# Layer 0's local means on GpSimd between weight splits, and token tiles dealt out among the first modulation groups, in a fused kernel of three transformer layers

## The chip, the cores and the metric

One core of one Trainium2 chip. The metric is the device time of one execution in microseconds (us). The kernel before was run three times: median 2811.88 us, 2800.17 to 2812.4 us.

## What is computed

Everything is float32. Two blocks follow each other on 512 tokens of width 1024 (with 256 context tokens in the first block). The first has two layers of adaptive norm, mixer and gated feed-forward; the second has one layer with three kinds of attention and a feed-forward. The change touches two places of layer 0:

```python
def adaln(cond, w, b):                      # cond: c, and c_ctx; w: 1024 x 6144
    m = jax.nn.silu(cond) @ w + b
    return [m[:, None, i * d:(i + 1) * d] for i in range(6)]

h = rmsnorm(x, g) * (1.0 + scale) + shift   # x: tokens and context, 768 in all

def multiscale_pool(u, w_grp, ch_scale):    # u: 256 of the columns of h @ w_in, 4 groups of 64
    ...                                     # windows of 2, 4, 8, 16 tokens
    d = (win_sum / count - ug).astype(u.dtype)
    y = jnp.einsum("btgc,gcd->btgd", d, w_grp).reshape(B, T, POOL_DIM)
    return y * ch_scale
```

The other columns of `h @ w_in` are 12 query heads and 4 key and value heads, which get a head norm and a rotary embedding before attention. `multiscale_pool` is the first part of what goes into the output projection.

## The kernel before

**Engines.** Each engine runs its own program in order; semaphores tie them. TensorE (PE) does all products. A float32 weight tile (1024 x 128, called a unit) lands in one of four slots of `raw`; ScalarE (ACT) rounds it to `whi` (`upper`, line 918), GpSimd (POOL) computes `wlo = raw - whi` (`lower`, line 782), and PE makes three matmuls per piece (lines 1376 to 1378; 1393 to 1395 for the first two units after a norm). POOL does little else in layer 0. SyncE (SP) issues the weight loads in the planned order, each when its slot of the ring is free. There are four PSUM groups `G[0..3]`, taken in turn by every step of the plan; a step waits until the engine that reads the group's last content has freed it (`gfree`).

**The opening.** PE computes the modulation in groups of 512 columns (`ada`, line 1409, four loads of 512 KB each, straight from `raw`), and turns each group's row into columns (`ada_turn`, line 1422), which Vector (DVE) takes with the bias (`ada_columns`, line 1806). Groups 0 to 3 of layer 0 come in the opening. The order is: group 0, the turned vectors (`vec`), all eight token tiles (`xin`: six transposes each, line 1721; DVE copies the tile into `xT`, line 2239; ACT squares it, line 933; DVE adds the square to `ssq`, line 1825), then groups 1, 2, 3. Then comes norm 0: PE sums `ssq` over partitions (line 1445), ACT takes the root (line 953), DVE the reciprocal (line 1833) and a diagonal (line 1835), PE spreads it (line 1452), DVE and ACT write the normed tiles. ACT's order there: squares, groups 1 to 3, `upper(0)`, `upper(1)`, root.

**The input stage `in0`.** Twelve units: 0 and 1 keys, 2 and 3 the 256 columns of the local means, 4 to 9 queries, 10 and 11 values. Beside units 0 to 7 one more modulation group each (groups 4 to 11) is computed. The plan of step n is:

```python
plan_unit((st, "U", n), ...)            # unit n: three matmuls per piece
plan_aux(("adaT",) + ada[n - 1])        # turn modulation group n-1
plan_ada(*ada[n])                       # modulation group n
... "V", n - 1 / "S", n - 1 / "R", n - 2    # values; sum of squares (head norm); rotation
```

For a query or key unit, ACT copies and squares the product (lines 993 and 997, freeing its PSUM group), PE sums the squares (line 1488), ACT takes the root (line 1012), DVE the reciprocal (line 1879) and the scaled copy (line 1883), PE rotates (line 1496), DVE combines (lines 1894, 1895, 1897).

The local means (`pooling`, lines 2268 to 2281) run on DVE as one block, called after its step n = 5: 22 chained additions, products and subtractions over `upad` (two tiles of 128 channels, 800 padded columns) into `dT`. PE needs them only after the twelve units, in the two products with `poolw` (line 1732); then come `pair_attention`, the output projection and the feed-forward.

Of the kernel before, what the change touches and what calls it, by code (L numbers as in the profile page):

```python
# [13 lines left out]
P = 128  # L14
# [90 lines left out]
def build(nc, A, out):  # L105
    with ExitStack() as ctx:
# [34 lines left out]
        eps = sb("eps", [P, 1])  # L141
        zero8 = sb("zero8", [P, KD])
# [416 lines left out]
        def stage_sems(st, *names):  # L559
            for n in names:  # L560
# [3 lines left out]
                   "silu", "b", "rope1", "icnt", "band", "steps", "cszero", "adasel", "halves", "tri")  # L564
        stage_sems("in0", "pooled", "pooly", "pooldone")
# [76 lines left out]
        def _(sp):  # L642
# [9 lines left out]
            with nc.allow_non_contiguous_dma(reason="small vectors"):  # L652
# [4 lines left out]
                sp.dma_start(mats[:], A["mats"][:, 0:8]).then_inc(PH["set", "cond"], 16)  # L657
# [106 lines left out]
        def _(pool):  # L764
# [95 lines left out]
            def causal_tables():  # L860
# [8 lines left out]
                for head in range(4, 6):  # L869
# [39 lines left out]
        def _(act):  # L909
# [17 lines left out]
            def residual_squares(i, ctx_too):  # L927
                n = T if ctx_too else TX
                for m in range(KD):
                    act.wait_ge(*when((f"res{i}", "x"), m + 1))  # L930
                    if m >= 2:
                        act.wait_ge(*when((f"res{i}", "ssq"), m - 1))
                    act.activation(sq[:, m % 2, 0:n], xT[:, m, 0:n], ACT.Square).then_inc(PH[f"res{i}", "sq"], 1)
# [213 lines left out]
            def wout(l, i, n):  # L1147
                for m in range(KD):
                    act.wait_ge(*product_of(("wout", l, m)))
                    upper(plan["wout", l, m][0] + 2)  # L1150
                    if l == 0 and m < len(ADA_WOUT0):
                        ada(*ADA_WOUT0[m])
                    residual_square(i, m, n)

            def ffn(l, chunks, ranges, last_i):
# [4 lines left out]
                for c, (f0, nf) in enumerate(chunks):  # L1160
# [44 lines left out]
                    for m in range(KD):  # L1205
# [6 lines left out]
                        if last and last_i is not None:  # L1212
                            residual_square(last_i, m, n)
# [46 lines left out]
            ada(0, 0)  # L1260
            residual_squares(0, True)
            act.wait_ge(*auxiliary("vec"))
# [1124 lines left out]
```

## Time and profile before

| | |
|---|---|
| median of 3 runs | 2811.88 us |
| range of the runs | 2800.17 to 2812.4 us |
| the profiled execution | 2806.05 us |
| its span | 2804.3 us |
| its mean granted TensorE clock | 0.959 |
| busy share PE / DVE / ACT / POOL | 92% / 40% / 32% / 27% |

The profile is of one execution; its span leaves out 1.75 us of the execution's own time. A row of a timeline gives when an instruction or a run of like ones began, how long it took, its engine and line, what it writes and reads, and in brackets the idle time of the engine before it and what ended that. "DVEq" and "ACTq" are the engines' sequencers, "PEld" the weight loads into the array.

### The profile page before, as it was taken

How to read it: one execution, taken by the hardware profiler on the slowest of the kernel's cores; microseconds unless marked ns; L12 is line 12 of the kernel's file. 1: busy time of each engine (PE TensorE's matmuls, PEld its weight loads, DVE VectorE, ACT ScalarE, POOL GpSimd, SP SyncE). 2: the span in 40 equal slices, each digit the busy share in tenths (PEclk: the TensorE clock that was granted, in tenths of full speed). 3: DMA queues.
4: the chain of work that ended last, by engine and by line, in shares of the span. 5: the costliest groups of instructions: out<-in, count | busy, mean ns of one | idle time of the engine just before them, and what ended most of it. 6: DMA issues, size and time to landing. Idle time of an engine off the chain costs nothing.

```text
span 2804.3 us, 34798 instructions
## 1 busy us (share of the span) xinstructions
PE 2589.0 (92%) x13587; PEld 2016.5 (72%) x13587; DVE 1128.4 (40%) x1578; ACT 910.0 (32%) x1460; POOL 756.7 (27%) x372
## 2 busy tenths in 40 slices
PE   5978999899999998997699988999989998799998
PEld 3656667688888885783277676888867865688887
DVE  4366641411121124347944644222246355434323
ACT  2224641321121223323344533222234365323322
POOL 1111002122222221320200113444444360344443
PEclk8999999899999998998899999999999998999999
DMA  6540017122222234210100112333323310233332
GB/s 240 174 134 24 1 32 222 48 60 67 60 61 67 60 111 133 77 27 20 55 9 8 34 32 74 98 98 98 90 82 83 89 37 1 61 98 97 98 96 77
DMA packets 345573, 212.58 MB, mean 76 GB/s; under 512 B 37747, under 2 KB 318669, under 8 KB 345442
## 3 DMA queue, kind: packets, MB, share of 16 engines
q1 hardware_dynamic: 328176, 200.97, 24.3%
q10 hardware_dynamic: 17202, 9.72, 1.2%
q8 instruction: 91, 1.49, 0.2%
q14 instruction: 40, 0.33, 0.0%
q0 software_dynamic: 64, 0.08, 0.0%
HBM read 208.58 MB, written 2.16 MB: 75 GB/s over the span
## 4 chain that ended last, share of the span: by engine, by line
PE 75%; DVE 9%; issue 7%; ACT 3%; DMA 3%; POOL 2%; ACTq 0%; SPq 0%; DVEq 0%; POOLq 0%
PE G L1376 19%; PE G L1377 19%; PE G L1378 18%; DVE scr L1879 3%; PE G L1517 2%; PE G L1560 2%; POOL wlo L782 2%; PE G L1536 2%; PE G L1588 2%; PE G L1573 2%; PE G L1527 1%; DMA raw<-in_l_ada_w_dram 1%; PE G L1488 1%; PE G L1409 1%; PE G L1393 1%
## 5 line engine op out<-in xcount | busy, mean ns | idle before, releaser
L782 POOL TENSOR_TENSOR wlo<-raw,whi 128x1024 fp32r<-128x1024 f32 x282 | 681.0, 2415 | 1800.2 <-ACT whi L918 1800.2
L1376 PE MATMUL G<-big_a,whi 128*128 128x512 f32 x2024 | 747.4, 369 | 28.9 <-DVE mod L1806 14.9
L1377 PE MATMUL G<-big_a,wlo 128*128 128x512 f32 x2024 | 734.4, 363 | 0.0
L1378 PE MATMUL G<-big_a,whi 128*128 128x512 f32 x2024 | 731.0, 361 | 0.0
L918 ACT ACTIVATE whi<-raw 128x1024 fp32r<-128x1024 f32 x282 | 298.9, 1060 | 1242.5 <-PE G L1378 1051.8
L1376 PEld LDWEIGHTS G<-big_a,whi 128*128 128x128 f32 x2024 | 383.6, 190 | 106.9 <-issue 29.4
L1377 PEld LDWEIGHTS G<-big_a,wlo 128*128 128x128 f32 x2024 | 383.4, 189 | 63.8 <-issue 6.2
L1378 PEld LDWEIGHTS G<-big_a,whi 128*128 128x128 f32 x2024 | 382.3, 189 | 60.6
L1376 PE MATMUL G<-big_b,whi 128*128 128x512 f32 x832 | 307.5, 370 | 7.3 <-DVE big_b L2194 3.5
L1377 PE MATMUL G<-big_b,wlo 128*128 128x512 f32 x832 | 306.6, 368 | 0.0
L1378 PE MATMUL G<-big_b,whi 128*128 128x512 f32 x832 | 305.4, 367 | 0.0
L1879 DVE RECIPROCAL scr<-scr 128x512 f32<-128x512 f32 (+3 forms) x50 | 201.2, 4023 | 159.6 <-ACT scr L1012 158.8
L2177 DVE TENSOR_TENSOR scr<-G,scr 128x768 f32<-128x768 f32 (+1 forms) x44 | 36.3, 825 | 436.2 <-PE G L1378 422.7
L2131 DVE SCALAR_TENSOR_TENSOR xT<-G,mod,xT 128x512 f32<-128x512 f32 (+1 forms) x96 | 60.6, 659 | 358.6 <-PE G L1378 358.6
L1376 PEld LDWEIGHTS G<-big_b,whi 128*128 128x128 f32 x832 | 156.7, 188 | 41.4 <-DVE big_b L2194 5.2
L1378 PEld LDWEIGHTS G<-big_b,whi 128*128 128x128 f32 x832 | 156.4, 188 | 26.7
L1377 PEld LDWEIGHTS G<-big_b,wlo 128*128 128x128 f32 x832 | 156.7, 188 | 25.5
L2182 DVE TENSOR_TENSOR big_b<-scr,big_b 128x768 f32 (+3 forms) x44 | 99.8, 2269 | 46.4 <-ACT big_b L1178 46.4
L2190 DVE TENSOR_TENSOR scr<-scr 128x512 f32<-128x512 f32 x32 | 79.9, 2497 | 65.7 <-ACT scr L1190 65.7
L2129 DVE TENSOR_TENSOR xT<-G,xT 128x512 f32 (+1 forms) x40 | 27.7, 692 | 173.9 <-PE G L1378 162.4
L1081 ACT ACTIVATE scr<-scr,stat 128x768 f32<-128x768 f32 (+4 forms) x136 | 91.1, 674 | 8.0 <-DVE scr L1966 6.3
L1560 PE MATMUL G<-plain_b 64*128 64x256 f32 (+3 forms) x368 | 76.8, 519 | 12.7 <-DVE scr L1966 5.8
(234 smaller groups left out, 2833.2 us busy)
## 6 DMA issues: line engine op xcount, KB each, us to landing
raw<-in_l_ada_w_dram SPq DMA_DIRECT2D x96, 512.0 KB, 5.3
raw<-in_l_ffn_w_gate_dram SPq DMA_DIRECT2D x44, 512.0 KB, 3.9
raw<-in_l_ffn_w_up_dram SPq DMA_DIRECT2D x44, 512.0 KB, 3.8
raw<-in_l_ffn_w_down_dram SPq DMA_DIRECT2D x32, 512.0 KB, 3.6
raw<-in_w_up_dram SPq DMA_DIRECT2D x32, 512.0 KB, 4.0
raw<-in_w_down_dram SPq DMA_DIRECT2D x32, 512.0 KB, 4.1
raw<-in_w_in_dram SPq DMA_DIRECT2D x28, 512.0 KB, 3.8
raw<-in_l_w_in_dram SPq DMA_DIRECT2D x24, 512.0 KB, 3.9
```

Source lines behind the costliest of these rows:

```text
L782: pool.tensor_tensor(wlo[:, u % 2], raw[:, r % RING], whi[:, u % 2].bitcast(F32), ALU.subtract).then_inc(raw_free[r % RING], 1)
L918: act.activation(whi[:, u % 2], raw[:, r % RING], ACT.Copy).then_inc(hi_done, 1)
L1081: act.activation(p, p, ACT.Exp, bias=stat[:, 0, c:c + 1], scale=-1.0, accum_out=stat[:, 1, c:c + 1]).then_inc(PH[C.st, "prob"], 1)
L1376: pe.matmul(o, whi[:, u % 2, k], rlo[:, k, t0:t0 + w], start=k == 0, stop=False)
L1377: pe.matmul(o, wlo[:, u % 2, k], rhi[:, k, t0:t0 + w], start=False, stop=False)
L1378: mm = pe.matmul(o, whi[:, u % 2, k], rhi[:, k, t0:t0 + w], start=False, stop=k == k_tiles - 1)
L1517: mm = pe.matmul(o, un["q"], kt, start=True, stop=fox is None)
L1560: mm = pe.matmul(C.scores(n, h)[:, c0:c0 + wk], heads[h]["q"], kt, start=True, stop=True)
L1879: release(dve.reciprocal(rs, rs), key)
L2131: ins = dve.scalar_tensor_tensor(out=x, in0=src, scalar=gate(m, q, j, dyn), in1=x, op0=ALU.mult, op1=ALU.add)
L2182: dve.tensor_tensor(alo[:, tile_at(j, 2, b), 0:n], sq[:, b:b + 1, 0:n], ahi[:, tile_at(j, 2, b), 0:n].bitcast(F32), ALU.subtract).then_inc ...
L2190: dve.tensor_tensor(sq[:, b % 2, 0:n], qr[:, b % 2, 0:n], qr[:, b % 2, 0:n], ALU.mult).then_inc(PH[sems, "prod"], 1)
```

## The change

Three edits.

1. The 22 operations of the local means go from DVE to POOL, each waiting for the one before by a new semaphore `in0_pooling`. They are dealt out between the weight splits: two (window sums of tile 0) after `lower(6)`, four after `lower(7)`, six after `lower(8)`, two after `lower(9)`, four after `lower(10)` and four after `lower(11)`, with the semaphore `in0_pooled` set at the end. DVE's block disappears.
2. In the opening the eight token tiles are dealt out: tiles 0 and 1 after modulation group 0, 2 to 4 after group 1, 5 to 7 after group 2, none after group 3, on PE, ACT and DVE alike. On SP only the identity (64 KB) is loaded first; the other seven matrices of `mats` (448 KB) follow the loads of group 0.
3. `root_table()`, a root of one column into `spare`, is put ahead of the first use of each norm's root: in the opening ahead of `upper(0)`, elsewhere beside the first tile of the stage before the norm.

```diff
+        XIN_AFTER = ((0, 1), (2, 3, 4), (5, 6, 7), ())
         for i in range(4):
             plan_ada(0, i)
-            if i == 0:
-                plan_aux("vec")
-                for m in range(KD):
-                    plan_aux(("xin", m))
-            else:
-                plan_aux(("adaT", 0, i - 1))
+            plan_aux(("adaT", 0, i - 1) if i else "vec")
+            for m in XIN_AFTER[i]:
+                plan_aux(("xin", m))
...
-                sp.dma_start(mats[:], A["mats"][:, 0:8]).then_inc(PH["set", "cond"], 16)
+                sp.dma_start(ident, A["mats"][:, 0]).then_inc(PH["set", "cond"], 16)
...
+                sp.dma_start(mats[:, 1:8], A["mats"][:, 1:8]).then_inc(PH["set", "mats"], 16)
...
+            pool_steps = [0]
+
+            def pooled(ins):
+                pool_steps[0] += 1
+                ins.then_inc(PH["in0", "pooling"], 1)
+                pool.wait_ge(PH["in0", "pooling"], pool_steps[0])
+
+            L = UPW
+            pa, pb = ptmp[:, 0], ptmp[:, 1]
+
+            def window_sums(i):
+                u = upad[:, i]
+                pooled(pool.tensor_tensor(pa[:, 1:L], u[:, 1:L], u[:, 0:L - 1], ALU.add))
+                pooled(pool.tensor_tensor(pb[:, 2:L - 1], pa[:, 1:L - 2], pa[:, 3:L], ALU.add))
+
+            def wider_sums():
+                pooled(pool.tensor_tensor(pa[:, 4:L - 3], pb[:, 2:L - 5], pb[:, 6:L - 1], ALU.add))
+                pooled(pool.tensor_tensor(pb[:, 8:L - 7], pa[:, 4:L - 11], pa[:, 12:L - 3], ALU.add))
+
+            def window_means(i, half):
+                rows = slice(HD * half, HD * half + HD)
+                sums = pb if half else pa
+                for t0, w, p0 in ((0, TX, 8), (TX, TC, 24 + TX)):
+                    d = dT[rows, i, t0:t0 + w]
+                    pooled(pool.tensor_tensor(d, sums[rows, p0:p0 + w], d, ALU.mult))
+                    pooled(pool.tensor_tensor(d, d, upad[rows, i, p0:p0 + w], ALU.subtract))
+
             for u in range(0, first["wout", 0, 0] + 2):
                 lower(u)
+                if u == 6:
+                    for i in range(2):
+                        key = ("in0", "U", L0_POOL[i])
+                        pool.wait_ge(gfree[group_of(key) % 4], group_of(key) // 4 + 1)
+                    pool.wait_ge(*when(("set", "icnt"), 16))
+                    window_sums(0)
+                if u in (7, 8, 10, 11):
+                    pool.wait_ge(raw_free[unit_ring[u] % RING], unit_ring[u] // RING + 1)
+                if u in (7, 8):
+                    window_means(0, u - 7)
+                if u == 8:
+                    window_sums(1)
+                if u == 9:
+                    wider_sums()
+                if u in (10, 11):
+                    window_means(1, u - 10)
+                if u == 11:
+                    pool.sem_inc(PH["in0", "pooled"], 1)
...
+            def root_table():
+                act.activation(spare[:], eps[:], ACT.Sqrt)
...
-            ada(0, 0)
-            residual_squares(0, True)
-            act.wait_ge(*auxiliary("vec"))
-            act.dma_start(halves[0:12], A["mats"][0:12, 8]).then_inc(PH["set", "halves"], 16)
-            for i in range(1, 4):
+            for i in range(4):
                 ada(0, i)
+                if i == 0:
+                    act.wait_ge(*auxiliary("vec"))
+                    act.dma_start(halves[0:12], A["mats"][0:12, 8]).then_inc(PH["set", "halves"], 16)
+                for m in XIN_AFTER[i]:
+                    residual_square(0, m, T)
+            root_table()
             upper(0)
             upper(1)
...
+            for i in range(4):
+                if i:
+                    ada_columns(0, i - 1)
+                for m in XIN_AFTER[i]:
...
+            sum_squares(0, KD - 1, T)
+            ada_columns(0, 3)
             modulation_gain(0, 0)
...
-            inputs("in0", S0, L0_V, 12, v0_tile, {5: pooling}, ADA_IN0)
+            inputs("in0", S0, L0_V, 12, v0_tile, None, ADA_IN0)
```

**On POOL, in `in0`.** `wlo` rows are the splits of units; the rows on `plain_b` are the new work (window sums on 128 partitions, means on 64). From the split of unit 8 to that of unit 10, before:

```order
L782 TENSOR_TENSOR wlo<-raw,whi 128x1024 x20
```

and now:

```order
L782 TENSOR_TENSOR wlo<-raw,whi 128x1024
L902 TENSOR_TENSOR plain_b<-plain_b 64x512
L903 TENSOR_TENSOR plain_b<-plain_b 64x512
L902 TENSOR_TENSOR plain_b<-plain_b 64x256
L903 TENSOR_TENSOR plain_b<-plain_b 64x256
L890 TENSOR_TENSOR plain_b<-plain_b 128x799
L891 TENSOR_TENSOR plain_b<-plain_b 128x797
L782 TENSOR_TENSOR wlo<-raw,whi 128x1024
L894 TENSOR_TENSOR plain_b<-plain_b 128x793
L895 TENSOR_TENSOR plain_b<-plain_b 128x785
L782 TENSOR_TENSOR wlo<-raw,whi 128x1024
```

The run of 20 splits is cut after the seventh; this is its densest stretch, with six operations between the splits of units 8 and 9 and two between those of 9 and 10.

**On PE, in the opening.** `raw,cs` is a modulation group, `adasel,arow` its turn, `mats,plain_a` the transposes of token tiles (six each), `mats,ssq` norm 0. Before:

```order
L1721 MATMUL G<-mats,plain_a 128x128 x48
L1409 MATMUL G<-raw,cs 32x512 x8
L1422 MATMUL G<-adasel,arow 128x2 x4
L1409 MATMUL G<-raw,cs 32x512 x8
L1422 MATMUL G<-adasel,arow 128x2 x4
L1409 MATMUL G<-raw,cs 32x512 x8
L1422 MATMUL G<-adasel,arow 128x2 x8
L1445 MATMUL G<-mats,ssq 128x1 x6
```

and now (line numbers of the changed file):

```order
L1767 MATMUL G<-mats,plain_a 128x128 x12
L1455 MATMUL G<-raw,cs 32x512 x8
L1468 MATMUL G<-adasel,arow 128x2 x4
L1767 MATMUL G<-mats,plain_a 128x128 x18
L1455 MATMUL G<-raw,cs 32x512 x8
L1468 MATMUL G<-adasel,arow 128x2 x4
L1767 MATMUL G<-mats,plain_a 128x128 x18
L1455 MATMUL G<-raw,cs 32x512 x8
L1468 MATMUL G<-adasel,arow 128x2 x8
L1491 MATMUL G<-mats,ssq 128x1 x6
```

Groups 1 and 2 have moved ahead of six and three of the eight tiles.

**On ACT, ahead of norm 0.** `arow` is a modulation group's copy, `whi<-raw` the split of units 0 and 1. Before:

```order
L942 ACTIVATE arow<-G 128x512 x3
L918 ACTIVATE whi<-raw 128x1024 x2
L953 ACT_TABLE_LOAD
L953 ACTIVATE scr<-G,eps 128x6
```

and now:

```order
L988 ACTIVATE scr<-xT 128x768 x3
L982 ACTIVATE arow<-G 128x512
L973 ACT_TABLE_LOAD
L973 ACTIVATE spare<-eps 128x1
L963 ACTIVATE whi<-raw 128x1024 x2
L993 ACTIVATE scr<-G,eps 128x6
```

The table load stands ahead of the two splits, and the last three squares stand ahead of the copy of group 3.

## Rows read from the trace of the kernel before

**Rows 1.** The page: busy time, share of span and count of each engine.

```profile
PE 2589.0 (92%) x13587; PEld 2016.5 (72%) x13587; DVE 1128.4 (40%) x1578; ACT 910.0 (32%) x1460; POOL 756.7 (27%) x372
```

**Rows 2.** Windows: length, busy us of PE, PEld, DVE, ACT, POOL, clock, DMA share, GB/s.

```profile
140.00:160.00 20.00, 20.00 (x128) 14.86 (x127) 7.08 (x5) 4.73 (x7) 3.93 (x2) 1.00 0.61 185
160.00:180.00 20.00, 5.07 (x15) 3.39 (x14) 19.17 (x23) 2.96 (x4) 2.69 (x1) 0.67 0.43 130
```

**Rows 3.** Waits of PE between 140 and 245 us: total, times, longest.

```profile
PE G L1376 <- DVE mod L1806: 14.9, 1, 14.9
```

**Rows 4.** Timeline of DVE: start us, us, the work.

```profile
158.94 0.99 DVE L2268 TENSOR_TENSOR plain_b<-plain_b 128x799 f32<-128x799 f32 x1
...
176.59 0.17 DVE L1806 TENSOR_TENSOR mod<-G,vcol 128x8 f32<-128x8 f32 x1
```

**Rows 5.** The chain that ended last, 176 to 213 us: start us, us, what.

```profile
176.90 0.77 PE G L1376
...
187.16 0.79 PE G L1422 x8
...
203.59 0.40 PE G L1376
...
212.16 1.29 PE G L1488 x4
```

**Rows 6.** Timeline of POOL, 160 to 240 us.

```profile
164.24 2.69 POOL L782 TENSOR_TENSOR wlo<-raw,whi 128x1024 fp32r<-128x1024 f32 x1 [10.06 <-ACT whi L918]
194.50 2.40 POOL L782 TENSOR_TENSOR wlo<-raw,whi 128x1024 fp32r<-128x1024 f32 x1 [27.57 <-ACT whi L918]
...
235.42 2.34 POOL L782 TENSOR_TENSOR wlo<-raw,whi 128x1024 fp32r<-128x1024 f32 x1 [8.17 <-ACT whi L918]
```

**Rows 7.** Groups of POOL's instructions by form: busy us, mean ns.

```profile
L852 POOL TENSOR_TENSOR plain_a<-scr,vrow 128x128 f32<-128x128 f32 x24 | 11.0, 457 | 13.6 <-DVE scr L2048 13.6
```

**Rows 8.** Timeline of POOL: two instructions linked by a semaphore.

```profile
2265.05 1.27 POOL L842 TENSOR_TENSOR plain_a<-plain_a,arow 128x512 f32<-128x512 f32 x1
2266.40 1.49 POOL L841 TENSOR_SCALAR plain_a<-arow 128x512 f32<-128x512 f32 x1
```

**Rows 9.** DVE's line 1895: duration ns min/median/max, first and last start us.

```profile
L1895 DVE TENSOR_TENSOR rt<-plain_b,rope x8: 681/682/2572, 121.4 to 235.7; 128x512 f32<-128x512 f32 x8
```

**Rows 10.** Timeline of DVE, around 200 us.

```profile
200.71 1.02 DVE L1883 SCALAR_TENSOR_TENSOR plain_b<-scr,vcol 128x768 f32<-128x768 f32 x1
```

**Rows 11.** Timeline of ACT, around 202 us.

```profile
202.53 0.80 ACT L997 ACTIVATE scr<-G 128x768 f32<-128x768 f32 x1
```

**Rows 12.** Timeline of PE in the opening.

```profile
23.31 6.49 PE L1721 MATMUL G<-mats,plain_a 128*128 128x128 f32 x42
...
32.86 1.93 PE L1409 MATMUL G<-raw,cs 128*32 128x512 f32 x16 [1.18 <-DVEq L633]
...
38.08 5.80 PE L1409 MATMUL G<-raw,cs 128*32 128x512 f32 x16 [2.05 <-DMA raw<-in_l_ada_w_dram]
...
50.64 1.95 PE L1422 MATMUL G<-adasel,arow 128*128 128x2 f32 x16
```

**Rows 13.** Window of the opening (columns as in rows 2).

```profile
27.00:35.00 8.00, 5.61 (x48) 3.65 (x47) 6.98 (x9) 3.56 (x5) 0.00 (x0) 1.00 0.01 5
```

**Rows 14.** Timeline of DVE in the opening.

```profile
24.84 0.96 DVE L2239 COPY xT<-G 128x768 f32<-128x768 f32 x1 [0.34 <-PE G L1721]
...
39.14 2.02 DVE L1825 TENSOR_TENSOR ssq<-ssq,scr 128x768 f32<-128x768 f32 x2 [0.23 <-DVE xT L2239]
...
56.66 0.19 DVE L1833 RECIPROCAL scr<-scr 128x6 f32<-128x6 f32 x1
```

**Rows 15.** The page: the weight split's first half on ACT.

```profile
L918 ACT ACTIVATE whi<-raw 128x1024 fp32r<-128x1024 f32 x282 | 298.9, 1060 | 1242.5 <-PE G L1378 1051.8
```

**Rows 16.** Timeline of ACT: table load of norm 0; root of norm 1.

```profile
54.71 1.28 ACT L953 ACT_TABLE_LOAD   x1
...
501.14 0.27 ACT L953 ACTIVATE scr<-G,eps 128x6 f32<-128x6 f32 x1 [4.93 <-PE G L1445]
```

More of the change, by code:

```diff
@@ L141, in build @@
         eps = sb("eps", [P, 1])
+        spare = sb("spare", [P, 1])
         zero8 = sb("zero8", [P, KD])
@@ L925, in link @@
                 act.wait_ge(act_step, chain[0])
[L927 to L933, printed above, removed]
+            def root_table():
+                act.activation(spare[:], eps[:], ACT.Sqrt)
             def ada(l, i):
@@ L1709, in _ @@
                     ada_turn(0, i - 1)
-                    continue
-                pe.wait_ge(*when(("set", "tables"), 32))
-                pe.wait_ge(*when(("set", "rows"), 16 * 24))
-                a, g = plan["vec"]
-                pe.transpose(G[g % 4][:, 0:P], vrow[:, 0, :], ident)
-                aux(pe.transpose(G[g % 4][:, P:P + VROWS2], vrow[0:VROWS2, 1, :], ident[0:VROWS2, 0:VROWS2]))
-                pe.wait_ge(*when(("set", "xload"), 32))
-                for m in range(KD):
+                else:
+                    pe.wait_ge(*when(("set", "tables"), 32))
+                    pe.wait_ge(*when(("set", "rows"), 16 * 24))
+                    a, g = plan["vec"]
+                    pe.transpose(G[g % 4][:, 0:P], vrow[:, 0, :], ident)
+                    aux(pe.transpose(G[g % 4][:, P:P + VROWS2], vrow[0:VROWS2, 1, :], ident[0:VROWS2, 0:VROWS2]))
+                    pe.wait_ge(*when(("set", "xload"), 32))
+                for m in XIN_AFTER[i]:
                     a, g = plan["xin", m]
@@ L1722, in _ @@
                     aux(mm)
+            pe.wait_ge(*when(("set", "mats"), 16))
             ada_turn(0, 3)
@@ L2234, in _ @@
             free(dve, "vec")
-            for m in range(KD + 1):
-                if m < KD:
+            for i in range(4):
+                if i:
+                    ada_columns(0, i - 1)
+                for m in XIN_AFTER[i]:
                     key = ("xin", m)
@@ L2241, in _ @@
                     free(dve, key)
-                if m >= 1:
-                    sum_squares(0, m - 1, T)
-            for i in range(4):
-                ada_columns(0, i)
+                    if m >= 1:
+                        sum_squares(0, m - 1, T)
+            sum_squares(0, KD - 1, T)
+            ada_columns(0, 3)
             modulation_gain(0, 0)
@@ L2257, in v0_tile @@
                 dve.sem_inc(PH["in0", "vdone"], 1)
-            def pooling():
-                for i in range(2):
-                    key = ("in0", "U", L0_POOL[i])
-                    dve.wait_ge(gfree[group_of(key) % 4], group_of(key) // 4 + 1)
-                dve.wait_ge(*when(("set", "icnt"), 16))
-                L = UPW
-                for i in range(2):
-                    u, a, b = upad[:, i], ptmp[:, 0], ptmp[:, 1]
-                    link(dve.tensor_tensor(a[:, 1:L], u[:, 1:L], u[:, 0:L - 1], ALU.add))
-                    link(dve.tensor_tensor(b[:, 2:L - 1], a[:, 1:L - 2], a[:, 3:L], ALU.add))
-                    if i == 0:
-                        tiers = ((0, a), (1, b))
-                    else:
-                        link(dve.tensor_tensor(a[:, 4:L - 3], b[:, 2:L - 5], b[:, 6:L - 1], ALU.add))
-                        link(dve.tensor_tensor(b[:, 8:L - 7], a[:, 4:L - 11], a[:, 12:L - 3], ALU.add))
-                        tiers = ((0, a), (1, b))
-                    for half, s in tiers:
-                        rows = slice(HD * half, HD * half + HD)
-                        for t0, w, p0 in ((0, TX, 8), (TX, TC, 24 + TX)):
-                            d = dT[rows, i, t0:t0 + w]
-                            link(dve.tensor_tensor(d, s[rows, p0:p0 + w], d, ALU.mult))
-                            link(dve.tensor_tensor(d, d, u[rows, p0:p0 + w], ALU.subtract))
-                dve.sem_inc(PH["in0", "pooled"], 1)
-            inputs("in0", S0, L0_V, 12, v0_tile, {5: pooling}, ADA_IN0)
+            inputs("in0", S0, L0_V, 12, v0_tile, None, ADA_IN0)
             for i in range(2):
```

8 lines of the change are left out of this document (6 added, 2 removed).

## The prediction

> **What bounds the kernel now.** I first read the page's busy shares: PE is busy 92% of the span, the others 40% or less [rows 1]. So a change pays only where PE stands, and I looked for those places in the two stages that the diff touches. The windows by stage show one: from 140 to 160 us PE is busy all of the time, from 160 to 180 it is busy for 5.07 us of 20, while DVE is busy for 19.17 [rows 2]. The waits of PE name it: one wait of 14.9 us, ended by DVE's line 1806, which takes a modulation group's columns and frees its PSUM group [rows 3]. The timeline of DVE shows what stood before that instruction: the block of local means, from 158.94 us to the start of line 1806 at 176.59 [rows 4]. So PE waits for a 0.17 us instruction queued behind 17.6 us of work that nobody needs before the twelve units are done. The second place is the opening, up to norm 0's reciprocal at 56.66 us [rows 14]. There PE transposes eight tiles first (from 23.31 us on) and reaches modulation group 1 at 32.86 [rows 12], although its weights had landed by then: from 27 to 35 us the DMA engines are at 1% [rows 13]. Group 2 can be asked for only when group 1 has emptied the ring's slots.
>
> **Part 1: the block leaves DVE.** Without it line 1806 follows DVE's last step at about 159, and unit 7 starts when PE is ready, at 176.90 - 14.9 = 162.0 us. That gives back 14.9 us. Unit 7 also ran slowly after the idle time: from its first matmul at 176.90 to the turn at 187.16 it took 10.26 us, unit 9 from 203.59 to 212.16 only 8.57 [rows 5]. With no idle time before it, I count the 1.7 us as gained too. What is late next? In the same DVE step comes the reciprocal of unit 5's head norm, which waits for ACT's root and, through ACT, for the weights of unit 8. In the steps before and after the block this chain keeps PE full (the window from 140 to 160, and unit 9 right behind ACT's square in step 8), so I expect it to do so here.
>
> **Part 2: the block arrives on POOL.** No such operation is in POOL's rows at 799 or 256 columns. An addition of 128 columns takes 0.457 us [rows 7] and one of 512 takes 1.27 [rows 8]: 0.186 us plus 2.12 ns a column, which gives 2.36 for 1024, where the splits take 2.34 to 2.40 [rows 6]. So 799 columns cost 1.88 and 256 columns 0.73; I assume that 64 partitions cost as much as 128. The next instruction of a linked pair begins 0.08 us after the end of the one before (2265.05 + 1.27 to 2266.40) [rows 8]. The 22 operations are six of full width at 1.95 with the gap, eight of 512 at 1.35 and eight of 256 at 0.81: 11.7 + 10.8 + 6.5 = 29.0 us, where DVE needed 17.6. Is there room? The densest stretch follows the split of unit 8, at 164.24 us [rows 6]: six operations, 8.2 us, from 166.6 to 174.8. The split of unit 9 came at 194.50 [rows 6], so now at 194.5 - 16.6 = 177.9, and PE needs it only at 203.59 - 16.6 = 187.0. POOL is 3 us early and could be another 6.7 late. The splits are some 10.2 us apart (194.50 to 235.42, four intervals) [rows 6], so that of unit 11 begins near 215.0 - 16.6 = 198.4, and the last means end near 205; PE's products with `poolw`, which wait for them, stand beside the split of 235.42, so near 219. So the work itself is hidden: cost 0. If POOL had no such gaps, all 29 us would lie on PE's path.
>
> What is not hidden is DVE's contact with POOL. Line 1895 takes 0.682 us in the median and 2.572 at most, and that maximum began at 235.7 [rows 9], beside the split at 235.42 that ran to 237.76 [rows 6]: DVE waited for POOL's instruction and lost 1.89 us. The Trainium skill, "SBUF — State Buffer", section "Who interferes with whom", says that a Vector instruction with two inputs in SBUF and a GpSimd instruction that reads SBUF exclude each other for a whole instruction; by this rule, the trace agrees. Lines 1883, 1895 and 1897 are of this kind. It matters where the chain has no slack. In step 8, line 1883 starts at 200.71 [rows 10], ACT's copy and square follow and end at 203.33 [rows 11], and unit 9, which needs the group that they free, starts at 203.59 [rows 5]. POOL's two wider sums, put after the split of unit 9 (194.50 + 2.40), would end at 196.9 + 3.9 = 200.8 in the same clock, 0.1 us into line 1883. In the other steps ACT copies a product without waiting for line 1883, or waits for weights after it, so there is more slack. Ends: 0, if nothing overlaps on the path; 9.5 us, if in each of the steps 7 to 11 one full wait of 1.89 lies on it. I take 0.5, nearest to the overlap worked out for step 8.
>
> **Part 3: the opening.** DVE needs 2.04 us a tile (first copy at 24.84, last sum ends at 39.14 + 2.02 = 41.16, eight tiles) [rows 14]. Now group 1 follows the second tile, at about 26. From group 1 to the end of group 2 took 38.08 + 5.80 - 32.86 = 11.0 us, mostly the ring waiting for its loads [rows 12]; so group 2 ends near 37.0. Tiles 2 to 4 and their DVE work lie inside that. Then come a turn (1.95 us for two, so 1.0) and the transposes of tile 5 (6.49 us for 42, so 0.9) [rows 12], DVE starts on it near 39.0 and has copied the last tile near 45. Group 3 is loaded meanwhile. ACT is next in line: last square at 45.1, copy of group 3 (0.6, estimated from the 0.80 of a wider copy) [rows 11], table load 1.28 [rows 16], root of `spare` 0.27, two splits at 1.06 [rows 15], root 0.27 [rows 16]: 49.6, and the reciprocal at 49.7 instead of 56.66: 6.9 us gained. The diagonal behind it (line 1835, two SBUF inputs) now falls beside the split of unit 0, and I take off 0.4: **6.5 us**. Ends: 3 us, if the loads of group 2 land 3.5 later than by this spacing; 11 us, if DVE never stands (41.2 plus 4.5 of ACT).
>
> **Part 4: the root's table.** The load of 1.28 us stands on the path only at norm 0, and is in part 3. At norm 1 the root waited 4.93 us for PE with its table already there [rows 16]; the same holds for later norms, and ACT has room for the extra 0.27. Gain 0, cost 0. Loading the identity first moves 448 KB behind group 0; the bytes up to group 1 are the same, so 0.
>
> **The sum.** 14.9 + 1.7 - 0.5 + 6.5 = 22.6 us. Against the profiled execution, 2806.05 - 22.6 = 2783.5. That execution was 5.8 us under the median of the runs, and the place of the gain does not depend on it, so against the median: 2811.9 - 22.6 = 2789.3. I predict **2789 us**.
>
> **The rivals.**
> *A, the port takes much of it back.* For: the new operations fill POOL exactly in the steps where DVE does three two-input operations each, and the chain of step 8 has a tenth of a microsecond to spare. Against: the other steps have more, and a wait ends with one short operation. Time: 9.5 us instead of 0.5, 2789.3 + 9.0 = 2798.
> *B, the opening gives nothing.* The token tiles now stand behind modulation weights, so DVE stands twice, while before it worked without a gap. If group 1's loads land late, the reciprocal stays near 56. Against: DMA was idle for 8 us. Time: 2811.9 - 16.1 = 2796.
> *C, it doesn't do what it says.* If unit 7's group were held by something else than DVE's block, the 14.9 us would stay: 2811.9 - 6.5 = 2805. Against: in the timeline PE starts 0.3 us after line 1806 [rows 4, 5].
> *D, slower: POOL is too slow and becomes the engine that PE waits for.* The place is the splits of units 9 to 11 and `in0_pooled`. From the split of unit 8 (164.2) to PE's need of the means (219) POOL has 55 us, less four splits of 2.4: 45 us for the 16 operations that stand there, 2.8 us each. Past that every microsecond lands on PE, and the change loses when they take (45 + 23) / 16 = 4.2 us each, three times my mean of 1.3; at 5 us each the time is 2789.3 + 80 - 45 = 2824. Against: the rows for 128, 512 and 1024 columns lie on one line. The Trainium skill, "GPSIMD Engine Reference", section "Elementwise — side-by-side cycle accounting", speaks against the change as well: it finds an addition of 2048 columns 1.96 times slower there than on Vector and keeps elementwise work on Vector. My ratio, 29.0 to 17.6, is no better; but what counts here is whose queue is waited for.
>
> **How the numbers follow.** Forecast 0.70, A 0.12, B 0.12, C 0.03, D 0.03. A measurement of this kernel can tell about 0.5%, 14 us, from no change: under 2797.8 is faster. The forecast lies there almost whole (0.68), of B two thirds (0.08), of A some 0.05: faster 0.81. C and the rest of A and B are the same, 0.16; D is slower, 0.03. The range: best case 16.6 + 11 = 27.6 us off the fastest run shown, 2800.2, is 2773, and I stop at 2774; upwards it takes in B and A with 4 us for the spread of the runs: 2802.
>
> **What would show it.** Right: no row of the new kind on POOL over 2.2 us when nothing stands in its way; PE busy all through the window that held 5.07; unit 7 in 8.6 us; the reciprocal of norm 0 near 50; the gain by the end of unit 11 near 23 us, and no change in the lengths of later stages. Wrong: PE waiting for POOL's `wlo` or for `in0_pooled`; line 1883 or 1895 at 2 us or more in steps 7 to 11 with PE idle behind it; token tiles copied later than 45.

## The result and the profile after

The changed kernel takes 2782.98 us (median of 5 runs, 2778.25 to 2786.83), the kernel before, run beside it, 2809.87 (5 runs, 2800.17 to 2812.4). The ratio is 0.9906, 95% interval [0.9884, 0.9928], so some 26 us less, between 20 and 33. The forecast was 22.6 us less. The profiled execution took 2782.98 us too, with a span of 2781.2 where it was 2804.3.

The page of the changed kernel, busy shares [rows 1]:

```profile
PE 2583.1 (93%) x13587; PEld 2015.9 (72%) x13587; DVE 1110.4 (40%) x1556; ACT 911.4 (33%) x1466; POOL 785.4 (28%) x394
```

The 22 instructions left DVE (1578 to 1556), arrived on POOL (372 to 394) and brought 28.7 us of busy time there, for 18.0 less on DVE. PE does the same 13,587 instructions. So the gain can only be idle time of PE (17.2 us of the 23.1 that the span is shorter) and the same matmuls at a better clock (its busy time fell by 5.9 us, the mean granted clock rose from 0.959 to 0.962). The windows show where (columns as in [rows 2]; the first line answers to [rows 13]):

```profile
27.00:35.00 8.00, 7.19 (x48) 3.48 (x46) 4.29 (x7) 2.73 (x4) 0.00 (x0) 1.00 0.85 280
140.00:160.00 20.00, 20.00 (x117) 15.61 (x116) 9.52 (x4) 6.19 (x8) 10.53 (x8) 1.00 0.76 226
160.00:180.00 20.00, 19.36 (x110) 14.22 (x109) 15.14 (x13) 7.21 (x9) 12.77 (x9) 1.00 0.59 153
180.00:200.00 20.00, 20.00 (x104) 16.02 (x103) 15.83 (x10) 5.13 (x6) 13.37 (x10) 1.00 0.17 52
```

From 140 to 200 us PE now stands for 0.64 us in all, and POOL, at 0.5 to 0.7 of its time, is never what it waits for. The DMA engines, at 1% before in the window from 27 to 35, are at 85%. The waits of PE from 125 to 245 us have no entry of 14.9 [rows 3] any more. A wait on the same pair of lines is left, 0.6 us long and one step later, for group 10's columns and not group 9's:

```profile
PE G L1606 <- DVEq L632: 4.5, 1, 4.5
...
PE G L1422 <- DVE mod L1853: 0.6, 1, 0.6
```

For the accounts below I use marks that each trace has. The turn of a modulation group on PE comes once a step; here are those of groups 9, 10 and 11, before and then after:

```profile
156.83 0.95 PE L1422 MATMUL G<-adasel,arow 128*128 128x2 f32 x8
187.00 0.95 PE L1422 MATMUL G<-adasel,arow 128*128 128x2 f32 x8
200.39 0.95 PE L1422 MATMUL G<-adasel,arow 128*128 128x2 f32 x8
```

```profile
148.21 0.95 PE L1468 MATMUL G<-adasel,arow 128*128 128x2 f32 x8
161.59 0.95 PE L1468 MATMUL G<-adasel,arow 128*128 128x2 f32 x8
175.86 0.95 PE L1468 MATMUL G<-adasel,arow 128*128 128x2 f32 x8
```

Group 9 to 10 took 30.17 us and takes 13.38: 16.8 less. Group 10 to 11 took 13.39 and takes 14.27: 0.9 more. The end mark is the start of the last value copy, 238.95 before and 214.27 after: 24.7 us gained. "The stretch" below is from DVE's taking of group 4's columns (91.59 before, 83.25 after) to that mark: 147.4 before, 131.0 after, 16.3 less. The opening, to norm 0's reciprocal, gives the other part: 56.66 before, 48.51 after, 8.15 less (0.2 more comes between).

Behind the input stage the lead wanders: at the reciprocals of norms 1 to 5 it is 26.3, 29.4, 25.8, 25.6 and 26.2, at the end 23.1. The program is the same there but for the root's table, and the runs of one kernel differ as much among themselves. I give no cause for these plus or minus 3 us.

### The profile page after: what moved, and what is told of

Its sections match the earlier page's. It is cut to its first block, busy times and chain, and to the rows that moved or that the text cites. A ratio compares the mean times of both kernels' runs of the same rounds, so it can differ in the third digit from the quotient of the medians.

```text
span 2781.2 us, 34811 instructions
## 1 busy us (share of the span) xinstructions
PE 2583.1 (93%) x13587; PEld 2015.9 (72%) x13587; DVE 1110.4 (40%) x1556; ACT 911.4 (33%) x1466; POOL 785.4 (28%) x394
## 4 chain that ended last, share of the span: by engine, by line
PE 77%; DVE 8%; issue 7%; ACT 3%; DMA 2%; POOL 2%; SPq 0%; DVEq 0%; ACTq 0%; POOLq 0%
PE G L1422 19%; PE G L1423 19%; PE G L1424 19%; DVE scr L1926 3%; PE G L1563 2%; PE G L1606 2%; PE G L1582 2%; POOL wlo L782 2%; PE G L1619 2%; PE G L1634 2%; DMA raw<-in_l_ada_w_dram 2%; PE G L1573 1%; PE G L1534 1%; PE G L1455 1%; PE G L1439 1%
## 5 line engine op out<-in xcount | busy, mean ns | idle before, releaser
L1424 PEld LDWEIGHTS G<-big_b,whi 128*128 128x128 f32 x832 | 156.7, 188 | 26.9
L2176 DVE TENSOR_TENSOR xT<-G,xT 128x512 f32 (+1 forms) x40 | 27.7, 692 | 174.8 <-PE G L1424 164.1
```

The source lines that it names most:

```text
L1424: mm = pe.matmul(o, whi[:, u % 2, k], rhi[:, k, t0:t0 + w], start=False, stop=k == k_tiles - 1)
```

## The experiments

"Before" in the table is the profiled execution; times with a ratio are medians of runs beside the kernel before, and "one run" is the single run that was profiled. The marks of the last four columns are from the profiled execution of each kernel: norm 0's reciprocal, the two distances between turns, and the stretch.

| kernel | time | ratio, interval | reciprocal | 9 to 10 | 10 to 11 | stretch |
|---|---|---|---|---|---|---|
| before | 2806.05 | | 56.66 | 30.17 | 13.39 | 147.4 |
| the change | 2782.98 | 0.9906 [0.9884, 0.9928] | 48.51 | 13.38 | 14.27 | 131.0 |
| means_only | 2792.0 | 0.9949 [0.9932, 0.9965] | 59.20 | 13.38 | 14.21 | 131.3 |
| opening_only | 2799.05 | 0.9968 [0.9955, 0.9981] | 48.94 | 30.28 | 13.39 | 148.2 |
| dealt_on_dve | 2782.59 | 0.9914 [0.9887, 0.994] | 48.55 | 13.54 | 13.38 | 130.9 |
| block_on_pool | 2801.42 | one run | 48.53 | 13.80 | 33.05 | 150.5 |
| dealt_early | 2783.65 | 0.9918 [0.9901, 0.9934] | 48.09 | 14.31 | 13.38 | 131.9 |
| means_x2 | 2787.43 | one run | 51.98 | 13.77 | 13.38 | 135.0 |
| means_x3 | 2813.43 | one run | 50.04 | 14.50 | 15.50 | 155.4 |
| no_root_table | 2786.71 | one run | 50.66 | 13.38 | 14.16 | 132.1 |
| matrices_first | 2786.2 | 0.9926 [0.9906, 0.9946] | 53.02 | 13.59 | 14.25 | 131.3 |

**means_only**: the kernel before with edit 1 alone.

```diff
-            inputs("in0", S0, L0_V, 12, v0_tile, {5: pooling}, ADA_IN0)
+            inputs("in0", S0, L0_V, 12, v0_tile, None, ADA_IN0)
```

(and on POOL the 22 operations as in the change.)

> The kernel before with the local means on POOL, dealt out as in the change; opening and root table as before. The marker is the start of the last copy of value tiles on DVE, the end of the input stage: 238.95 us before, 214.27 in the change. Theory (the parts add up, and this one is the 14.9 us wait plus the slow unit behind it, less a wait for the port of under 1 us): marker at 222.4, time 16.5 us under before, near 2793. Rival (the port takes much back): marker 229 or later, several operations of DVE at 2 us or more with PE idle behind them.

**opening_only**: the changed kernel with DVE's block back in step 5.

```diff
-            inputs("in0", S0, L0_V, 12, v0_tile, None, ADA_IN0)
+            inputs("in0", S0, L0_V, 12, v0_tile, {5: pooling}, ADA_IN0)
```

> The change with the local means back on DVE as one block after its step 5. Theory: norm 0's reciprocal at 48.5 us as in the change, the 14.9 us wait of PE is back, marker at 238.95 - 8.1 = 230.8, time near 2802. Rival (the opening's gain is lost again in the input stage, where the first units wait for weights): marker 234 or later.

The two parts add up. Means alone: 16.3 us off the median beside it, its stretch that of the change within 0.3 us. Opening alone: 9.3 us, with the reciprocal at 48.94, the old stretch, and the old wait in place:

```profile
PE G L1404 <- DVE mod L1835: 14.3, 1, 14.3
```

16.3 + 9.3 = 25.6 against 26.9 of the change: within the intervals, neither part feeds on the other. In the profiled run of means_only the reciprocal came at 59.20, 2.5 us later than in the kernel before with the same opening: the landing of its loads moves this mark between profiles, so I compare stretches rather than single ends.

**dealt_on_dve**: the same dealing out, but on DVE: after step 3 the sums and first means of tile 0; after step 4 its other means, both sums of tile 1 and its first means; after step 5 the rest.

```diff
-            inputs("in0", S0, L0_V, 12, v0_tile, None, ADA_IN0)
+            inputs("in0", S0, L0_V, 12, v0_tile, {3: means_3, 4: means_4, 5: means_5}, ADA_IN0)
```

> The change with the 22 operations on DVE after all, but dealt out: 6 after its step 3, 12 after step 4 (with the wider sums), 4 after step 5, where it stands idle. Theory (what cost was the block in front of the modulation columns, not the engine): no wait of PE over 1 us, marker at 213.4, 0.9 before that of the change since nothing meets POOL beside the rotations. Rival (the work has to leave DVE): steps 3 to 5 get longer, marker 219 or later.

The engine is not what mattered. With all 22 operations still on DVE, PE has no wait on DVE's columns, the stretch is 130.9 and the time 2782.59, the same as the change's within either interval. The operations need 0.99, 0.69 and 0.42 us there, where POOL needs 1.52, 1.29 and 0.73. What cost 16 us was one block in one place of a queue. Two of them stood beside a split; one is this:

```profile
133.11 2.77 DVE L2313 TENSOR_TENSOR plain_b<-plain_b 64x512 f32<-64x512 f32 x1
```

**block_on_pool**: the change with all 22 operations in one piece after `lower(7)`.

```diff
-                if u == 6:
+                if u == 7:
...
-                if u in (7, 8):
-                    window_means(0, u - 7)
...
+                    for i in range(2):
+                        window_sums(i)
+                        if i:
+                            wider_sums()
+                        window_means(i, 0)
+                        window_means(i, 1)
```

> The change with all 22 operations in one block on POOL, after the split of unit 7. Theory (dealing out matters, as the splits wait in the same queue): the block runs from 145 to 174 us, the split of unit 8 follows at 174 instead of 155.7, the last load of modulation group 11 waits for its slot, and PE stands some 17 us there: marker near 232. Rival (POOL has so much idle time that order on it does not matter): marker 214 to 216.

On POOL the dealing out matters as much as it did on DVE. The first and the last rows of the block, and the split queued behind it, in POOL's timeline:

```profile
147.28 1.52 POOL L890 TENSOR_TENSOR plain_b<-plain_b 128x799 f32<-128x799 f32 x1 [0.17 <-POOL wlo L782]
...
175.43 0.72 POOL L903 TENSOR_TENSOR plain_b<-plain_b 64x256 f32<-64x256 f32 x1
176.33 2.34 POOL L782 TENSOR_TENSOR wlo<-raw,whi 128x1024 fp32r<-128x1024 f32 x1 [0.18 <-POOL plain_b L903]
```

The block takes 28.9 us (29.0 worked out), and the stretch is 19.5 us longer than in the change, some 3 longer than before; of the gain only the opening's is left. But PE's waits don't name POOL:

```profile
PE G L1450 <- DMA raw<-in_l_ada_w_dram: 16.9, 2, 16.6
```

The split of unit 8 is what empties its slot of the ring; the load of the next modulation weights stands behind that slot (SyncE waited up to 23.8 us at a time for POOL's split before it issued one), and PE behind the load. Who reads only the name "DMA" here would look for the fault in the wrong place.

**means_x2** and **means_x3**: each of the 22 operations is followed by one, or two, additions of its size into a spare strip, which nobody reads. The edit of means_x2 (means_x3 has 3 in place of both 2):

```diff
+                n = sizes[(pool_steps[0] - 1) // 2]
+                if pool_steps[0] % 2:
+                    pooled(pool.tensor_tensor(junk[0:n[0], 0:n[1]], upad[0:n[0], 0, 0:n[1]],
+                                              upad[0:n[0], 1, 0:n[1]], ALU.add))
```

> The change with each of POOL's 22 operations followed by one addition of the same size into scratch (44 operations, 2.6 us per original). Theory of a threshold (the room on POOL is 2.8 us per operation): nearly free, stretch 131 to 134, the splits of units 9 to 11 late by 5 to 6 us but ahead of PE's need; the rest is rotations waiting for the port. Rival (POOL's work is paid for in proportion, or the port takes it): stretch 140 or more.

> The change with each of POOL's 22 operations followed by two additions of the same size into scratch (66 operations, 3.9 us per original). Theory of a threshold: PE now waits for the splits of units 9, 10 and 11 and for the means, 18 us in all, stretch near 149 us, as long as before the change. Rival (in proportion): twice the loss of the run with one extra. Rival (no threshold, work on POOL stays free): 131 to 134.

This measures the room that rival D spoke of. In the change the 16 operations after the split of unit 8 fill 21.6 us between their splits, 1.35 each with their gap. The added ones are slower than the originals in part (1.9 us for 799 columns), so in means_x2 the 16 with their additions fill 46.0 us, 2.87 each: just past the 2.8 that I gave as the limit. It costs 4.0 us in the stretch. That is 135.0 where the theory had 131 to 134 and its rival 140 or more; the waits name a rotation on DVE with 1.3 and POOL's split with 0.3. In means_x3 they fill 68.2 us, 4.26 each: by D's rule 68.2 - 45 = 23 us, and the stretch is 24.4 longer (155.4, with 149 expected), with the wait that D named. Its one run, 2813.43, is no faster than the kernel before (2806.33 to 2809.87 beside it); D had put the point where the gain is used up at 4.2 us each:

```profile
PE G L1430 <- POOL wlo L783: 18.9, 3, 11.3
```

**dealt_early**: the operations one to three splits earlier, to take them out of DVE's way in steps 7 and 8.

```diff
-                if u == 6:
+                if u in (5, 6, 7, 8):
+                    pool.wait_ge(raw_free[unit_ring[u] % RING], unit_ring[u] // RING + 1)
+                if u == 5:
...
+                    window_means(0, 0)
+                if u == 6:
+                    window_means(0, 1)
...
+                if u == 7:
...
+                    window_means(1, 0)
                 if u == 8:
...
+                    window_means(1, 1)
```

> The change with POOL's 22 operations one split earlier and packed closer: 6 after the split of unit 5, 6 after 6, 6 after 7, 4 after 8. The stretch from DVE's taking of modulation group 4 to the last value copy is 147.4 us before and 131.0 in the change. Theory (in the change PE lost 0.9 us at unit 8 to rotations that waited for POOL's operations; in the earlier steps DVE has little to do): no rotation waits in the step of unit 8, no wait of PE for line 1853's counterpart, stretch 130.1, time within noise of the change, near 2782. Rival (POOL has no room there, splits come late): a split starts more than 1 us after its first half is ready, stretch 132 or more.

A miss: the stretch is 131.9 us, not 130.1. Group 10 to 11 is back at 13.38, as expected, but group 9 to 10 is now 14.31. In DVE's timeline the rotation of step 7 is at its usual 0.68 each, and the scaled copies ahead of it, a row of 1.02 us elsewhere, are long:

```profile
150.49 1.95 DVE L1930 SCALAR_TENSOR_TENSOR plain_b<-scr,vcol 128x768 f32<-128x768 f32 x1
...
162.99 1.42 DVE L1930 SCALAR_TENSOR_TENSOR plain_b<-scr,vcol 128x768 f32<-128x768 f32 x1
164.34 0.68 DVE L1941 TENSOR_TENSOR rt<-G,rope 128x512 f32<-128x512 f32 x1
```

It is the first of these that PE feels. ACT's copy and square of the product stand behind it (152.53 and 153.23), and PE's rotation waits for them:

```profile
154.23 1.10 PE L1542 MATMUL G<-plain_b,mats 128*128 128x512 f32 x2 [0.69 <-ACTq L632]
```

The contact moved by one step and kept its price of 0.9 us.

**no_root_table**: the change without edit 3; the table is loaded at the norm's root, as before.

```diff
-                act.activation(spare[:], eps[:], ACT.Sqrt)
+                return
```

> The change without the root of one column ahead of the norms. Theory of the prediction (the table load lies on the path at norm 0 only, 1.3 us): norm 0's reciprocal at 49.8 instead of 48.5, the other norms unchanged. Rival (in the changed opening the root waits for PE, so the load is covered; but both splits move 1.5 us forward and meet the gain of line 1862 and the cleared pad): the root itself is not later, the reciprocal moves by what the port costs, 49.4 or so. Rival (nothing): 48.5.

Here the group 3 weights landed some 1.1 us later than in the change, so I count from DVE's taking of group 3's columns to the reciprocal: 3.07 us in the change (45.44 to 48.51), 4.15 here (46.51 to 50.66). That is 1.1 us more, but not the load of 1.28: the load ended at 49.27, before PE's sums (46.65 + 2.72 = 49.37). ACT had its root by 49.67, and DVE was still busy, in its timeline:

```profile
46.51 0.16 DVE L1853 TENSOR_TENSOR mod<-G,vcol 128x8 f32<-128x8 f32 x1
46.71 2.13 DVE L1862 SCALAR_TENSOR_TENSOR amix<-mod,vcol 128x16 f32<-128x16 f32 x1
49.24 1.39 DVE L2298 MEMSET plain_b<- 128x1600 f32 x1 [0.40 <-DVE amix L1862]
50.66 0.19 DVE L1880 RECIPROCAL scr<-scr 128x6 f32<-128x6 f32 x1
```

An instruction of 16 columns, 0.17 us in the change, took 2.13, because the split of unit 0 had begun on POOL just before it:

```profile
46.45 4.66 POOL L782 TENSOR_TENSOR wlo<-raw,whi 128x1024 fp32r<-128x1024 f32 x2 [37.50 <-ACT whi L963]
```

Loading the table first holds back `upper(0)` and with it the split (46.72 in the change), until that instruction (45.63) is through. The rival of this run, the port, explains it. The early load doesn't guarantee that: in means_x2 and matrices_first, which have it, PE's turn of group 3 was slow (3.58 and 3.57 us), the instruction came late, met the split (1.89 us each) and the distance was 3.91. In the six other profiles with the new opening and the early load, where it took 0.17 to 0.18, the distance was 2.4 to 3.3. So the size of 1.1 is that of this pair of profiles; what all of them show is that the contact costs, not the load.

**matrices_first**: the change with all eight matrices loaded first again.

```diff
-                sp.dma_start(ident, A["mats"][:, 0]).then_inc(PH["set", "cond"], 16)
+                sp.dma_start(mats[:], A["mats"][:, 0:8]).then_inc(PH["set", "cond"], 16)
...
-                sp.dma_start(mats[:, 1:8], A["mats"][:, 1:8]).then_inc(PH["set", "mats"], 16)
...
-            pe.wait_ge(*when(("set", "mats"), 16))
```

> The changed kernel with one part undone: all eight matrices are loaded first, in one transfer of 512 KB, ahead of modulation group 0, as before the change; the later wait for the other seven is gone. My theory: the bytes up to group 1 are the same and DMA has idle time in the opening, so the order of these two loads is worth 0 to 0.5 us: norm 0's reciprocal stays 3.1 to 3.6 us behind DVE's taking of modulation group 3 (3.07 in the change), the first of PE's ada matmuls begins about 1 us later, and that is caught up by group 1 or 2; time as the change, 2783 us, reciprocal at 48.5 plus or minus 1.5. Rival: loading the identity first is what made the opening 1.5 us better than I had worked out (8.1 instead of 6.6). Then groups 0 to 3 all come 1.2 us or more later, the reciprocal stands at 50 and the time at 2784.5. The loads' landings have moved the reciprocal by 1 to 3 us between runs, so only the start of PE's first group, the spacing of groups 0 to 3 and what each waits for can tell the two apart, not the time.

In this pair of profiles my theory fell: the delay is not caught up. PE's rows of group 1's first part, group 2's last and group 3's last, here and then in the change:

```profile
26.65 2.07 PE L1454 MATMUL G<-raw,cs 128*32 128x512 f32 x12
...
35.84 1.05 PE L1454 MATMUL G<-raw,cs 128*32 128x512 f32 x4 [0.23 <-DMA raw<-in_l_ada_w_dram]
...
43.84 1.73 PE L1454 MATMUL G<-raw,cs 128*32 128x512 f32 x4 [0.31 <-DMA raw<-in_l_ada_w_dram]
```

```profile
25.50 2.11 PE L1455 MATMUL G<-raw,cs 128*32 128x512 f32 x12
...
34.58 1.05 PE L1455 MATMUL G<-raw,cs 128*32 128x512 f32 x4 [0.23 <-DMA raw<-in_l_ada_w_dram]
...
42.41 1.05 PE L1455 MATMUL G<-raw,cs 128*32 128x512 f32 x4 [0.30 <-DMA raw<-in_l_ada_w_dram]
```

Here every group is 1.15 to 1.4 us later than in the change. But the change's profile is one of eight with the identity first, and they differ among themselves as much: the turn of group 1 begins between 28.7 and 29.9 us in them (29.9 here), that of group 2 between 34.9 and 37.1 (36.8 here). The one mark that separates the two orders is PE's transposes of the small vectors behind group 0: they begin at 22.4 to 22.9 us in the eight, at 23.6 here, and at 23.0 and 24.2 in the two kernels with the old opening, which load all eight matrices first too. Group 1 stands behind them on PE (its first row, 26.65, has no wait for a load). So a delay at the head is seen, but how much of it reaches the reciprocal is not shown. The reciprocal is 4.5 us later here, more than any group. The rest has two visible parts: the last four matmuls and the turn ran at the lower clock (1.73 us for 1.05, and 3.57 for 1.95; granted clock 0.51 from 44 to 52 us, 0.62 in the change), and with the turn late the small instruction on DVE met the split again (1.89 us). Both are in means_x2 as well, with the identity first (reciprocal at 51.98), so they don't belong to the order of the loads. The medians, 2786.2 and 2782.98, differ by 3.2 us, and their intervals overlap. The rival is the likelier of the two, and no more.

No version beat the change by more than the runs differ.

## Why the prediction was right, step by step

**What bounds the kernel.** Right: PE's two idle places, and the slow unit behind the first, are what the change gave back (24.7 us at the end mark). PE's instructions are the same.

**Part 1, the block leaves DVE: 16.6 forecast, 16.8 measured** (group 9 to 10). Rival C is dead: with the block gone the wait went, with the block back (opening_only) it was back. The clock's share was as expected too: of the 30.17 us, 14.9 was the wait and 13.4 is what the step takes now, which leaves 1.9 for the slow unit, 1.7 forecast.

**Part 2, the block on POOL: hidden, as forecast.** The total was 27.7 us busy and 22 gaps of 0.08, 29.5 for the 29.0 forecast. That is luck, two errors that cancel, as the rows show (POOL's timeline in the densest stretch):

```profile
155.73 2.41 POOL L782 TENSOR_TENSOR wlo<-raw,whi 128x1024 fp32r<-128x1024 f32 x1 [6.21 <-ACT whi L963]
158.22 1.29 POOL L902 TENSOR_TENSOR plain_b<-plain_b 64x512 f32<-64x512 f32 x1
...
162.58 2.11 POOL L890 TENSOR_TENSOR plain_b<-plain_b 128x799 f32<-128x799 f32 x1
164.77 1.84 POOL L891 TENSOR_TENSOR plain_b<-plain_b 128x797 f32<-128x797 f32 x1
```

The means are as forecast (1.28 to 1.29 and 0.72 to 0.73, for 1.27 and 0.73). The full-width operations need 1.51 to 1.52 undisturbed (at 133.17, 134.76 and 171.49, and in block_on_pool), not 1.88: the line through 128 and 512 columns does not hold for them, though it met the split's 1024. One of the six is an exception, the last wider sum (L895, 785 columns): 1.88 at 173.08, and 1.86 to 1.88 in five other profiles too, in means_x3 at 201.67 with DVE idle. So that is its own time; no run here says why. What stands above these times, 0.3 to 0.6 each in four operations of the 22, is contact with DVE. POOL still waited for ACT before every split.

**The port: 0.5 forecast at the wrong place, 0.9 measured at another.** I had put it in step 8, at DVE's line 1883. That instruction (now 1930) took 1.02 and 1.10 us in steps 8 and 9. The contact is in step 7, in DVE's timeline:

```profile
156.90 4.95 DVE L1926 RECIPROCAL scr<-scr 128x768 f32<-128x768 f32 x1 [6.48 <-ACT scr L1052]
161.89 1.42 DVE L1930 SCALAR_TENSOR_TENSOR plain_b<-scr,vcol 128x768 f32<-128x768 f32 x1
163.24 0.68 DVE L1941 TENSOR_TENSOR rt<-G,rope 128x512 f32<-128x512 f32 x1
163.84 1.40 DVE L1942 TENSOR_TENSOR rt<-plain_b,rope 128x512 f32<-128x512 f32 x1
165.27 1.89 DVE L1944 TENSOR_TENSOR plain_b<-rt 128x512 f32<-128x512 f32 x1
167.08 0.15 DVE L1853 TENSOR_TENSOR mod<-G,vcol 128x8 f32<-128x8 f32 x1
...
176.82 0.68 DVE L1942 TENSOR_TENSOR rt<-plain_b,rope 128x512 f32<-128x512 f32 x1
```

1.42, 1.40 and 1.89 stand for 1.02, 0.68 and 0.69: 2.3 us lost, beside POOL's operations from 160.96 to 166.6. They push the modulation columns, which I had cleared of the block but not of this, to 167.08, and PE starts unit 8 just behind, in the chain that ended last:

```profile
165.27 1.89 DVE plain_b L1944
...
167.38 0.47 PE G L1422
```

Of the 2.3 us PE feels 0.6 as a wait and the step 0.9; the rest was slack. The Trainium skill, "SBUF — State Buffer", section "Who interferes with whom", has a Vector instruction with two SBUF inputs and a GpSimd instruction exclude each other for a whole instruction; the trace agrees (1.40 and 1.89 us for 0.68 and 0.69). L1941, which reads one input from PSUM, stays at 0.68 in every row here, and between the short linked operations on POOL DVE gets in after one of them. That kept rival A at 0.9 us: each loss here, 0.4 to 1.2, is less than one operation of 1.3 to 2.1 us. That the two are tied is shown by which kernels have the 0.9: means_only, no_root_table and matrices_first, with POOL's operations in the same places, have it (14.16 to 14.25), opening_only and dealt_on_dve, without them, don't (13.39 and 13.38). It takes more than operations in the same places, though: in means_x2 the three rows of step 7 lost 1.1 us together, the columns were taken at 169.97, 3.6 us after the turn began (5.5 in the change), and the step has its 13.38.

**Part 3, the opening: 6.5 forecast, 8.15 measured.** The 8.15 is to the reciprocal, for which I had 6.9 before I took off 0.4 for what follows it. Rival B is dead, and the term was undersized, in two steps. (a) Group 2 ended at 35.6, not at the 37.0 of my sum, so DVE began tile 5 at 37.36 and not near 39.0, and the last square ended at 43.30 and not at 45.1. I had put loading the identity first at 0, as "the bytes up to group 1 are the same". Without it group 2 ends at 36.9 (35.84 + 1.05), so it may be worth up to 1.3 us of this; as said above, the profiles don't separate that from their own spread. (b) "ACT is next in line." It was not, neither before nor in the change. The chain that ended last in the kernel before, around norm 0:

```profile
52.62 0.18 DVE mod L1806
...
52.82 2.02 DVE amix L1815
...
55.23 1.40 DVE plain_b L2249
...
56.66 0.20 DVE scr L1833
```

It was DVE, held up by the split that began on POOL at 52.45, and then by a memset; ACT's root had ended at 56.28, 0.3 us before. The row was there to be read: a 16-column instruction of 2.02 us. In the change the same stretch of the chain has ACT's root behind PE's sums:

```profile
45.57 2.50 PE G L1491 x12
...
48.09 0.28 ACT scr L993
...
48.51 0.20 DVE scr L1880
```

There ACT stood 0.6 us for PE's sums, which took 2.48 us at a granted clock of 0.56 (1.48 at 1.00 before). So in the change neither ACT nor DVE came last but PE, which reaches its sums only after group 3's weights and two turns; that path was not in my sum. From the end of the last square to the reciprocal it took 5.2 us, where I had 4.6. In dealt_early and block_on_pool, where the sums took 1.6 and 1.8, ACT's root did not wait for PE, as I had forecast.

The 8.15 us are 7.18 up to DVE's taking of group 3's columns (52.62 to 45.44) and 0.97 from there on (4.04 to 3.07). The 0.4 us that I took off for the diagonal beside the split were 0.1 (1.15 for 1.05); there POOL waited, not DVE (two splits in 5.37 us). And DVE did copy tile 5 before my 39.0, at 37.36.

**Part 4, the root's table: 0 forecast, 1.1 measured in one pair of profiles.** My sum in part 3 kept the load of 1.28 us on ACT's path, ahead of the splits instead of behind them, so that moving it gained nothing. Without the early load the distance is 1.1 us longer, not because of the load, which is covered by PE's sums, but because the split then meets DVE's small instruction. The way in which edit 3 helps was not in the prediction. At the later norms it shows nothing, as forecast.

**Rival D** was rightly small: at the real price POOL has twice the room it needs (2.8 us for 1.35), and at 4.26 us each the rival's case came about. Beside that: the Trainium skill, "GPSIMD Engine Reference", section "Elementwise — side-by-side cycle accounting", finds an addition of 2048 columns 1.96 times slower on GpSimd. Here it is 1.52 to 0.99, 1.29 to 0.69 and 0.73 to 0.42, so 1.5 to 1.9 times. The trace agrees that POOL is the slower engine, and the time shows that this alone decides nothing.

**The sum** was 16.6 - 0.5 + 6.5 = 22.6; with the measured terms 16.8 - 0.9 + 8.15 = 24.1, and 0.6 of small differences in other steps makes the 24.7 at the end mark. Between that and the 26.9 of the medians lies nothing that the runs tell apart. Of the 6 us between the 2789 forecast and 2782.98, 2.0 are the kernel before, whose median was 2811.88 with three runs and 2809.87 with five.

## What to carry to other kernels

Read a queue, not an engine: work that nobody needs soon costs what stands behind it, so first ask whether it can be cut up and moved within its own queue; a slower engine will do as well if its gaps are cut to the same measure, and the same block there in one piece gives that gain back. Before you call one order of loads better than another, look how far the same marks lie apart in profiles with the same order: here one pair of profiles lay 1.15 to 1.4 us apart, and eight profiles with one order lay as far apart themselves. And an instruction far longer than its size explains (16 columns in 2 us) may be a neighbour's doing: look at what runs beside it before you name the engine that is "next in line", and at the same instruction with nothing beside it before you name the neighbour (785 columns in 1.88 us were not).

## What was not expected of the hardware

- A DVE instruction of 16 columns with two inputs in SBUF took 2.02 and 2.13 us beside a split of 2.4 on POOL, and 0.17 without one. Between no_root_table and the change, moving a table load by two instructions on a third engine decided which.
- POOL adds 799 columns on 128 partitions in 1.51 us, while 512 columns on 64 partitions take 1.29. The line through 128 and 512 columns gives 1.88 for 799, and no run here says why it is less. Nor why the sum of 785 columns takes 1.86 to 1.88 in the six profiles where no two-input instruction of DVE is beside it, or the added ones of 799 and 797 in means_x2 1.90 and 1.87 with DVE idle (138.89 and 142.46).
- The wait goes both ways. POOL's additions of 1.51 us grew to 2.11 and 1.84 beside DVE's two-input instructions, and the one of 1.88 to 2.46 in block_on_pool.
